# Moving one unit's scores ahead of another unit's products in TensorE's attention order

## The chip, the cores and the metric

The kernel runs on one core of one Trainium2 chip. The metric is the device time of one execution in microseconds (us); lower is better. Three runs of the kernel before are known, and one more execution was recorded by the hardware profiler. In what follows PE is TensorE's matmul row, PEld its weight-load row, DVE is VectorE, ACT is ScalarE, POOL is GpSimd, and SP issues the weight DMAs.

## The reference, cut to what matters

The model is a mixer block followed by two attention blocks, each with a feed-forward block. The change touches only the order of work inside the two attentions. In the first (called "nsa" in the kernel) the part in question is, for each of 16 heads, a masked softmax attention over 512 tokens, computed twice with two sets of keys and values (selected blocks and window; with 512 tokens both are causal attention over all earlier keys). In the second ("swa") it is attention in a band of 128 keys with one sink value per head.

```
def masked_softmax(s, mask):
    s = jnp.where(mask, s, -jnp.inf)
    m = jnp.max(s, axis=-1, keepdims=True)
    p = jnp.exp(s - m)
    d = jnp.sum(p, axis=-1, keepdims=True)
    return p / jnp.where(d > 0.0, d, 1.0)
...
    s = jnp.einsum('bgrqd,bgkd->bgrqk', q_blk, kb) * scale      # scores
    p = masked_softmax(s, mask)                                 # or with the sink in the sum
    o = jnp.einsum('bgrqk,bgkd->bgrqd', p, vb)                  # products with V
...
    o = gates[..., 0, None] * o_cmp + gates[..., 1, None] * o_slc + gates[..., 2, None] * o_win
```

## The kernel before

The whole model is one program, five engine queues written out by hand, with semaphores between them. Outside the attentions TensorE does long rows of 128x512 matmuls on weight tiles that SP streams in, ACT rounds (line 525) and POOL splits (line 494).

An attention is a list of units. A unit is one tile of 128 queries (index i) of one or two pairs of heads, with all key tiles that these queries see. The first attention has 48 units: 8 with one key tile, 8 with two, 16 with three and 16 with four; the first 16 have two pairs of heads, the others one. The second has 16 units of two pairs: 6 with two key tiles, 3 and then 1 with one, then 6 with two. The stages of a unit v and where they stand:

- S(v), function `score` (line 2149, in the second attention also the sinks, line 2153): TensorE multiplies queries with keys into two of the PSUM banks 2 to 5, by the unit's parity. It uses the array as two halves of 64 rows.
- maxima (line 1448), VectorE: adds the mask in place and takes the row maximum.
- E(v), function `exps` (line 799), ACT: exponentials out of PSUM into SBUF, with the row sums.
- T(v), function `turn` (line 2169), TensorE: transposes of the exponentials into banks 6 and 7, again in halves of 64 rows. Behind each half of T(v) stand the transposes W of the row weights of unit v-1 (line 2186).
- the copies of the transposes out of PSUM: bank 6 by VectorE (line 1458), bank 7 by ACT (line 811).
- row weights: VectorE's reciprocal (line 1465), POOL's product with the gates or its spread (lines 428 and 424).
- O(v), function `output` (line 2203), TensorE: V times the transposed exponentials into bank 0 or 1. It uses the array with 128 rows and 64 columns.
- the copy of the turned weights out of PSUM by ACT (line 818), then VectorE's product of output and weights (line 1474), then POOL's sum over branches and its split into high and low parts for the next linear layer.

The order of each queue is fixed. TensorE, in the steady state: T(v+1), O(v), S(v+3), T(v+2). VectorE: maxima(v+3), copy(v+2), reciprocal(v+2), output product(v). ACT: E(v+2), copy(v+1), weight copy(v), E(v+3). T(v+1) waits for E(v+1) and for both copies of unit v; O(v) waits for both copies of unit v; S(v+3) waits until E(v+1) has left its banks; ACT's weight copy(v) waits for O(v). In the second attention VectorE also has parts of the last query tiles between its first units (function `queries`).

The loop on TensorE that sets this order is the last one in `attention` (lines 2219 to 2231):

```
for v in range(v0, last):
    if v + 2 < last:
        score(v + 2)
    ...
    if v + 1 < last:
        turn(v + 1, None if first else v)
    if not first:
        output(v, v + 1 < last)
```

Of the kernel before, what the change touches and what calls it, by code (L numbers as in the profile page):

```python
# [143 lines left out]
def score_columns(i, swa):  # L144

    return P * len(key_tiles(i, swa)) + (1 if swa and i == 0 else 0)


def key_tiles(i, swa):

    return range(max(i - 1, 0), i + 1) if swa else range(i + 1)
# [21 lines left out]
def build(nc, a):  # L173
    with ExitStack() as ctx:
# [1489 lines left out]
        def _(pe):  # L1664
# [123 lines left out]
            def merged_part(stage, j, ks):  # L1788

                w, t = W0[stage] + j, T0[stage] + j  # L1790
                if ks[0] == 0:
                    wait_bank(t)
                    pe.wait_ge(tile_split, w)
                for k in ks:
                    pe.wait_ge(merged, MERGED[stage] + k + 1)
                    mm(psum(BANK[t]), WH[:, w % SPL, k], XH[:, k], start=(k == 0), stop=False)
                    mm(psum(BANK[t]), WH[:, w % SPL, k], XL[:, k], start=False, stop=False)
                    ins = mm(psum(BANK[t]), WL[:, w % SPL, k], XH[:, k], start=False, stop=(k == KT - 1))
                if ks[-1] == KT - 1:
                    ins.then_inc(tile_used, 1)  # L1800
# [327 lines left out]
            def attention(stage, units, v0, swa, lead=None, last_tile=None):  # L2128

                def score(v):  # L2130
                    c, pairs, m, i = units[v - v0]
                    js = key_tiles(i, swa)
                    n, k0 = score_columns(i, swa), P * js[0]
                    K = KS[:, 0] if swa else (KS, KW)[m][:, c // 4]
                    if v - v0 >= 2 or v >= 2 and not swa:
                        pe.wait_ge(p_exp, 2 * (v - 1))
                    if swa:
                        pe.wait_ge(*((q_last, 1) if c == 6 else (freed, T0["swa"] + 2 + c + pairs)))
                        pe.wait_ge(sink_ready, 1)
                    if swa and v == v0 + 1:  # L2140
                        pe.wait_ge(freed, T0["swa"] + 7)

                    s_ = [PS[:, 2 + 2 * (v % 2) + hh, 0:n * pairs].rearrange("p (r n) -> p r n", r=pairs) for hh in range(2)]
                    to = 1 if swa else 0
                    k1 = k0 + P * len(js)
                    for r in range(pairs):
                        for hh in range(2):
                            half = slice(DH * hh, DH * hh + DH)
                            ins = mm(s_[hh][:, r, to:n], QN[half, c + r, P * i:P * (i + 1)], K[half, k1 - n + to:k1],  # L2149
                                     start=(r == 0), stop=(r == pairs - 1 and not swa))  # L2150
                    for hh in range(2 if swa else 0):
                        half = slice(DH * hh, DH * hh + DH)
                        ins = mm(s_[hh][:, :, 0], oneb[half, 0:1].broadcast_to([DH, P]), sink_rows[half, 8 * hh + c:8 * hh + c + pairs],
                                 start=False, stop=True)
                    ins.then_inc(s_mm, 1)

                def turn(v, behind=None):
                    c, pairs, m, i = units[v - v0]
                    js, n = key_tiles(i, swa), score_columns(i, swa)
                    blocks = pairs * len(js)  # L2160
                    for hh in range(2):
                        pe.wait_ge(p_exp, 2 * v + hh + 1)
                        if v >= 1 and hh == 0:
                            pe.wait_ge(pt_d, v)
                            pe.wait_ge(pt_a, v)
                        for b in range(blocks):
                            at, to = n * (b // len(js) + 1) - P * (len(js) - b % len(js)), DH * (blocks * hh + b)
                            for q, rows_ in enumerate(HALVES):
                                ins = nc.tensor.transpose(PS[:, 6 + q, to:to + DH], PE_[rows_, v % 2, hh, at:at + P], ident[rows_, rows_])  # L2169
                        ins.then_inc(pt_mm, 1)  # L2170
                        if behind is not None:
                            if hh:
                                pe.wait_ge(w_half, behind + 1)
                            ins = turn_weight(behind, HALVES[hh])
                            if not hh:
                                ins.then_inc(w_half, 1)

                def turn_weight(v, rows_):
                    if v >= 2:
                        pe.wait_ge(o_done, v - 1)  # L2180
                    if last_tile and v < v0 + 2:
                        pe.wait_ge(freed, T0["swa"] + 9 + v - v0)
                    pe.wait_ge(w_ready, v + 1)
                    for r in range(units[v - v0][1]):
                        to = P * (2 + r)
                        ins = nc.tensor.transpose(PS[:, v % 2, to + rows_.start:to + rows_.stop], WN[rows_, v % 2, r], ident[rows_, rows_])
                    return ins

                def output(v, turned):
                    c, pairs, m, i = units[v - v0]  # L2190
                    pe.wait_ge(pt_d, v + 1)
                    pe.wait_ge(pt_a, v + 1)
                    if not turned:
                        turn_weight(v, slice(0, P)).then_inc(w_half, 1)
                    js = key_tiles(i, swa)
                    blocks = pairs * len(js)
                    for n, j in enumerate(js):
                        V = VW if (j < i if swa else m) else VS
                        for hh in range(2):
                            g = hh if swa else 2 * (c // 4) + hh  # L2200
                            pt = PT_[:, v % 2, :, DH * blocks * hh:DH * blocks * (hh + 1)].rearrange(
                                "p h (r j q) -> p j r h q", r=pairs, q=DH)
                            ins = mm(PS[DH * hh:DH * hh + DH, v % 2, 0:P * pairs].rearrange("p (r h q) -> p r h q", h=2, q=DH), V[:, j, g],  # L2203
                                     pt[:, n], start=(n == 0), stop=(n == len(js) - 1))
                    ins.then_inc(o_mm, 1)

                last = v0 + len(units)
# [6 lines left out]
                if last_tile:  # L2214
                    last_tile()
                    pe.wait_ge(freed, T0["swa"] + 8)
                    pe.wait_ge(tok_out, 6)
                    turn(v0)
                for v in range(v0, last):
                    if v + 2 < last:  # L2220
                        score(v + 2)
                    if v + 2 == last and not swa:
                        pe.wait_ge(p_exp, 2 * (last - 1))
                        merged_part(stage, 0, range(MERGED_PARTS[stage][0]))
                    first = v == v0 and not swa
                    if first:
                        output(v, False)
                    if v + 1 < last:
                        turn(v + 1, None if first else v)
                    if not first:  # L2230
                        output(v, v + 1 < last)
                early, most = MERGED_PARTS[stage]
# [34 lines left out]

            pe.wait_ge(cs_arg, NT)
            attention("nsa_o", NSA_UNITS, 0, False, last_chunk)
            pe.wait_ge(o_done, len(NSA_UNITS))  # L2270
            linear("nsa_o", first=2)
# [3 lines left out]
            pe.wait_ge(down_added, KT)  # L2275
            linear("swa", 9, 4, first=2)
            attention("swa_o", SWA_UNITS, len(NSA_UNITS), True, None, lambda: channel_major("swa", 9, 10))
            pe.wait_ge(o_done, len(NSA_UNITS) + len(SWA_UNITS))
            linear("swa_o", first=2)
# [142 lines left out]
```

## Time and profile before

| | us |
|---|---|
| median of 3 runs | 1599.99 |
| lowest, highest | 1599.51, 1605.58 |
| the profiled execution, whole | 1602.91 |
| its span, first to last instruction | 1601.1 |

The profiled execution is 2.92 us above the median of the runs. A sum made from its rows is taken off its span and, since nothing outside the span changes, off the median as well. Timeline rows are read as: start in us from the span's start, duration in us, engine, line, operation, output and inputs, the array's rows*columns for TensorE, the moving operand, the number of instructions merged into the row, and in brackets the idle time of that engine in front of the row with what ended it. The end of a matmul is modelled, so two matmul rows may overlap by some tenths of a us.

### The profile page before, as it was taken

Reading aid. Unit: us, or ns where it says so; the run is one execution under the profiler, and the core shown is the slowest. Engines: PE = TensorE matmul, PEld = TensorE weight load, DVE = VectorE, ACT = ScalarE, POOL = GpSimd, SP = SyncE. Lnnn points to the kernel's source line nnn. Section 1 sums busy time; section 2 is a strip of 40 time slices with the busy share of each in tenths; the row PEclk is TensorE's granted clock in tenths of the full one; section 3 lists DMA queues with packets and bytes.
Section 4 is the critical chain, followed back from the end, with each engine's and each line's share of the span. In section 5 each row is a group of like instructions: output and inputs, shape, how many; then the busy total and the mean of one; then the engine's idle time right before and its main releaser. Section 6 shows DMA issues by size and latency. Waiting matters only on the chain.

```text
span 1601.1 us, 21978 instructions
## 1 busy us (share of the span) xinstructions
PE 1571.9 (98%) x8401; PEld 1253.0 (78%) x8401; DVE 987.0 (62%) x1590; ACT 625.8 (39%) x1209; POOL 668.6 (42%) x486
## 2 busy tenths in 40 slices
PE   9999999999999999999999999999899999999997
PEld 7888757688888666688888888887668888888886
DVE  5999255567935677676655664457746756556444
ACT  4232334544633677542222222334754222223233
POOL 3444302054422464444444444444454444444443
PEclk9999999999999999999999999999999999999998
DMA  7322201043221000032322323323012232232231
GB/s 266 103 93 92 93 2 52 26 164 119 93 80 61 20 2 2 2 95 102 103 95 93 105 93 107 104 79 105 28 41 92 93 103 96 92 105 93 94 104 54
DMA packets 37817, 133.88 MB, mean 84 GB/s; under 512 B 4752, under 2 KB 5200, under 8 KB 37200
## 3 DMA queue, kind: packets, MB, share of 16 engines
q1 hardware_dynamic: 35840, 125.65, 23.4%
q10 hardware_dynamic: 1872, 6.82, 1.1%
q8 instruction: 68, 1.11, 0.3%
q14 instruction: 37, 0.30, 0.1%
HBM read 130.35 MB, written 2.10 MB: 83 GB/s over the span
## 4 chain that ended last, share of the span: by engine, by line
PE 85%; issue 6%; DVE 4%; ACT 2%; POOL 2%; DMA 0%; DVEq 0%; ACTq 0%; SPq 0%; POOLq 0%
PE ps L1721 17%; PE ps L1723 17%; PE ps L1722 17%; PE ps L2261 5%; PE ps L2263 5%; PE ps L2262 5%; PE ps L2149 2%; PE ps L2203 2%; ACT sb_arena L799 2%; PE ps L1710 1%; PE ps L2169 1%; PE ps L1853 1%; PE ps L1883 1%; PE ps L1906 1%; DVE sb_arena L978 1%
## 5 line engine op out<-in xcount | busy, mean ns | idle before, releaser
L494 POOL TENSOR_TENSOR sb_w_lo<-sb_raw,sb_w_hi 128x1024 fp32r<-128x1024 f32 x224 | 550.6, 2458 | 781.4 <-ACT sb_w_hi L525 734.9
L1721 PE MATMUL ps<-sb_x_hi,sb_w_hi 128*128 128x512 f32 x1280 | 501.8, 392 | 0.6 <-POOL sb_w_lo L494 0.6
L1723 PE MATMUL ps<-sb_x_hi,sb_w_lo 128*128 128x512 f32 x1280 | 498.2, 389 | 0.0
L1722 PE MATMUL ps<-sb_x_lo,sb_w_hi 128*128 128x512 f32 x1280 | 498.0, 389 | 0.0
L525 ACT CAST sb_w_hi<-sb_raw 128x1024 fp32r<-128x1024 f32 x226 | 238.0, 1053 | 637.8 <-PE ps L1723 432.8
L1721 PEld LDWEIGHTS ps<-sb_x_hi,sb_w_hi 128*128 128x128 f32 x1280 | 240.3, 188 | 52.8 <-issue 3.1
L1722 PEld LDWEIGHTS ps<-sb_x_lo,sb_w_hi 128*128 128x128 f32 x1280 | 240.3, 188 | 50.8 <-issue 1.4
L1723 PEld LDWEIGHTS ps<-sb_x_hi,sb_w_lo 128*128 128x128 f32 x1280 | 240.2, 188 | 49.9
L1542 DVE TENSOR_TENSOR sb_x_lo<-sb_arena,sb_x_hi 128x512 fp32r<-128x512 f32 x44 | 98.3, 2242 | 104.8 <-ACT sb_x_hi L864 104.8
L2263 PE MATMUL ps<-sb_x_hi,sb_w_lo 128*128 128x512 f32 x336 | 130.7, 389 | 0.0
L2261 PE MATMUL ps<-sb_x_hi,sb_w_hi 128*128 128x512 f32 x336 | 130.7, 389 | 0.0
L2262 PE MATMUL ps<-sb_x_lo,sb_w_hi 128*128 128x512 f32 x336 | 130.7, 389 | 0.0
L1550 DVE TENSOR_TENSOR sb_arena<-ps,sb_rstd 128x512 f32<-128x512 f32 x44 | 30.4, 691 | 154.7 <-PE ps L1723 154.7
L1554 DVE SCALAR_TENSOR_TENSOR sb_arena<-sb_arena,sb_cols 128x512 f32<-128x512 f32 x44 | 115.8, 2632 | 1.6
L799 ACT ACTIVATE sb_arena<-ps,sb_small 128x256 f32<-128x256 f32 (+4 forms) x192 | 94.0, 501 | 42.6 <-DVE sb_small L1448 34.5
L1448 DVE CUSTOM_DVE_ANT_0 ps<-ps,sb_arena 128x256 f32<-128x256 f32 (+4 forms) x192 | 82.9, 488 | 42.0 <-PE ps L2149 34.2
L859 ACT ACTIVATE sb_arena<-sb_arena 128x512 f32<-128x512 f32 x44 | 27.9, 633 | 150.5 <-DVE sb_arena L1556 150.4
L2263 PEld LDWEIGHTS ps<-sb_x_hi,sb_w_lo 128*128 128x128 f32 x336 | 63.1, 188 | 13.2
L2261 PEld LDWEIGHTS ps<-sb_x_hi,sb_w_hi 128*128 128x128 f32 x336 | 63.1, 188 | 13.0
L2262 PEld LDWEIGHTS ps<-sb_x_lo,sb_w_hi 128*128 128x128 f32 x336 | 63.1, 188 | 13.0
L2169 PEld LDWEIGHTS ps<-sb_ident,sb_arena 64*128 64x128 f32 x864 | 38.9, 141 | 43.8 <-ACT sb_arena L799 37.1
L2149 PE MATMUL ps<-sb_arena 64*128 64x128 f32 (+4 forms) x384 | 65.4, 449 | 0.1
(336 smaller groups left out, 2005.4 us busy)
## 6 DMA issues: line engine op xcount, KB each, us to landing
sb_raw<-in_w SPq DMA_DIRECT2D x227, 512.0 KB, 3.2
sb_arena<-in_cmp_w1k ACTq DMA_DIRECT2D x1, 2048.0 KB, 11.3
sb_arena<-in_cmp_w1v ACTq DMA_DIRECT2D x1, 2048.0 KB, 15.6
out<-sb_resid SPq DMA_DIRECT2D x6, 256.0 KB, 2.3
sb_resid<-in_x SPq DMA_DIRECT2D x5, 256.0 KB, 8.1
sb_arena<-in_pool_w SPq DMA_DIRECT2D x1, 1024.0 KB, 11.7
sb_arena<-in_invc SPq DMA_DIRECT2D x1, 1024.0 KB, 13.6
sb_resid<-in_x ACTq DMA_DIRECT2D x3, 256.0 KB, 7.4
```

Source lines behind the costliest of these rows:

```text
L494: nc.gpsimd.tensor_tensor(WL[:, w % SPL], raw[:, w % RAW], WH[:, w % SPL].bitcast(F32), ALU.subtract).then_inc(tile_split, 1)
L525: nc.scalar.copy(WH[:, w % SPL], raw[:, w % RAW]).then_inc(hi_made, 1)
L799: ins = nc.scalar.activation(PE_[:, v % 2, hh, n * r:n * (r + 1)], PS[:, 2 + 2 * (v % 2) + hh, n * r:n * (r + 1)], ACT.Exp, scale=-1.0, bi ...
L1542: nc.vector.tensor_tensor(XL[:, f % 4], MID[:, f], XH[:, f % 4].bitcast(F32), ALU.subtract).then_inc(xl_ready, 1)
L1554: step.mark(nc.vector.scalar_tensor_tensor(CV[:, b], AP_[:, b, 1:1 + S], w[1], CV[:, b], ALU.mult, ALU.add))
L1721: mm(out, WH[:, s, k], XH[:, k], start=(k == 0), stop=False)
L1722: mm(out, WH[:, s, k], XL[:, k], start=False, stop=False)
L1723: ins = mm(out, WL[:, s, k], XH[:, k], start=False, stop=(k == KT - 1))
L2149: ins = mm(s_[hh][:, r, to:n], QN[half, c + r, P * i:P * (i + 1)], K[half, k1 - n + to:k1], start=(r == 0), stop=(r == pairs - 1 and not swa))
L2261: mm(psum(k), WH[:, s, k], XH[:, x], start=False, stop=False)
L2262: mm(psum(k), WH[:, s, k], XL[:, x], start=False, stop=False)
L2263: ins = mm(psum(k), WL[:, s, k], XH[:, x], start=False, stop=(f == FT - 1))
```

## The change

TensorE's order inside both attentions changes; no operation is added or taken away, and no other engine's program changes. Before, the loop began a turn with the scores of unit v+2. Now the scores of the third unit stand ahead of the loop, and each turn issues the scores of unit v+3 right behind the transposes of unit v+1, in front of the products with V of unit v. In the steady state the order T(v+1), O(v), S(v+3) becomes T(v+1), S(v+3), O(v). In the first turn of the first attention O(0) already stands ahead of T(1), and there nothing moves. The last three turns of an attention have no scores left to issue.

```
@@ -2216,9 +2216,8 @@
                     pe.wait_ge(freed, T0["swa"] + 8)
                     pe.wait_ge(tok_out, 6)
                     turn(v0)
+                score(v0 + 2)
                 for v in range(v0, last):
-                    if v + 2 < last:
-                        score(v + 2)
                     if v + 2 == last and not swa:
                         pe.wait_ge(p_exp, 2 * (last - 1))
                         merged_part(stage, 0, range(MERGED_PARTS[stage][0]))
@@ -2227,6 +2226,8 @@
                         output(v, False)
                     if v + 1 < last:
                         turn(v + 1, None if first else v)
+                    if v + 3 < last:
+                        score(v + 3)
                     if not first:
                         output(v, v + 1 < last)
```

## Rows read from the trace of the kernel before

**Rows 1.** Waits of TensorE: line waiting, releaser: total us, times, longest.

```profile
PE ps L2169 <- ACT sb_arena L811: 13.6, 26, 2.4
```

**Rows 2.** Busy by stretch: length, then PE, PEld, DVE, ACT, POOL busy; clock, DMA.

```profile
544.42:552.05 7.63, 7.02 (x74) 4.68 (x73) 5.33 (x33) 6.04 (x30) 5.98 (x13) 0.90 0.02 3
552.05:577.97 25.92, 23.10 (x271) 15.04 (x270) 20.76 (x89) 21.27 (x81) 16.71 (x34) 1.00 0.01 2
583.29:617.99 34.70, 33.78 (x422) 22.33 (x422) 25.49 (x98) 24.93 (x85) 17.88 (x45) 1.00 0.01 3
617.99:661.96 43.97, 42.04 (x560) 27.53 (x557) 33.19 (x106) 31.23 (x90) 17.38 (x44) 1.00 0.01 2
...
1140.00:1149.00 9.00, 8.12 (x104) 5.52 (x100) 8.90 (x35) 7.39 (x29) 5.12 (x12) 1.00 0.01 4
...
1152.00:1159.56 7.56, 6.93 (x88) 4.70 (x83) 5.50 (x34) 6.10 (x31) 6.02 (x17) 1.00 0.01 3
1159.56:1178.84 19.28, 16.11 (x207) 11.12 (x204) 15.35 (x66) 15.82 (x61) 13.50 (x36) 1.00 0.09 30
```

**Rows 3.** Timeline, one loop of two units with two key tiles, first attention.

```profile
564.77 0.46 PE L2169 MATMUL ps<-sb_ident,sb_arena 64*128 64x64 f32 x8
...
565.65 1.08 PE L2203 MATMUL ps<-sb_arena 128*64 128x256 f32 x8
...
566.66 1.14 PE L2149 MATMUL ps<-sb_arena 64*128 64x256 f32 x8
...
568.81 0.47 ACT L799 ACTIVATE sb_arena<-ps,sb_small 128x256 f32<-128x256 f32 x1 [0.44 <-DVE sb_small L1448]
...
571.09 0.41 ACT L818 COPY sb_arena<-ps 128x256 f32<-128x256 f32 x1
...
571.37 0.46 PE L2169 MATMUL ps<-sb_ident,sb_arena 64*128 64x64 f32 x8
```

**Rows 4.** Timeline, the same loop for units with three key tiles.

```profile
583.29 0.40 PE L2169 MATMUL ps<-sb_ident,sb_arena 64*128 64x64 f32 x6
...
584.79 0.92 PE L2149 MATMUL ps<-sb_arena 64*128 64x384 f32 x4
...
586.47 0.58 ACT L799 ACTIVATE sb_arena<-ps,sb_small 128x384 f32<-128x384 f32 x1 [0.61 <-PE ps L2169]
...
587.34 0.92 PE L2149 MATMUL ps<-sb_arena 64*128 64x384 f32 x4
...
587.60 0.48 ACT L811 COPY sb_arena<-ps 128x384 f32<-128x384 f32 x1
...
588.22 0.40 PE L2169 MATMUL ps<-sb_ident,sb_arena 64*128 64x64 f32 x6
```

**Rows 5.** Timeline, the same loop for units with four key tiles.

```profile
626.69 0.46 PE L2169 MATMUL ps<-sb_ident,sb_arena 64*128 64x64 f32 x8 [0.22 <-ACT sb_arena L811]
...
628.47 1.13 PE L2149 MATMUL ps<-sb_arena 64*128 64x512 f32 x4
...
630.50 0.69 ACT L799 ACTIVATE sb_arena<-ps,sb_small 128x512 f32<-128x512 f32 x1 [1.03 <-DVE sb_small L1448]
...
632.57 0.46 PE L2169 MATMUL ps<-sb_ident,sb_arena 64*128 64x64 f32 x8 [0.22 <-ACT sb_arena L811]
```

**Rows 6.** Timeline, scores with transposes close behind them.

```profile
579.86 0.92 PE L2149 MATMUL ps<-sb_arena 64*128 64x384 f32 x4
...
580.61 0.35 PE L2169 MATMUL ps<-sb_ident,sb_arena 64*128 64x64 f32 x6
```

**Rows 7.** Timeline, the first two full-array matmuls behind scores, second attention.

```profile
1125.25 0.50 PE L1721 MATMUL ps<-sb_x_hi,sb_w_hi 128*128 128x512 f32 x1
1125.59 0.40 PE L1722 MATMUL ps<-sb_x_lo,sb_w_hi 128*128 128x512 f32 x1
```

**Rows 8.** Timeline, start of the second attention.

```profile
1134.97 0.46 PE L2169 MATMUL ps<-sb_ident,sb_arena 64*128 64x64 f32 x8 [2.43 <-ACT sb_arena L811]
...
1137.65 1.05 ACT L525 CAST sb_w_hi<-sb_raw 128x1024 fp32r<-128x1024 f32 x1
```

More of the change, by code:

```diff
@@ L2218, in attention @@
                     turn(v0)
+                score(v0 + 2)
                 for v in range(v0, last):
-                    if v + 2 < last:
-                        score(v + 2)
                     if v + 2 == last and not swa:
@@ L2229, in attention @@
                         turn(v + 1, None if first else v)
+                    if v + 3 < last:
+                        score(v + 3)
                     if not first:
```

## The prediction

> **What bounds the kernel now.** I read three views, from coarse to fine. First the waits of TensorE: nearly all that it waits for by name is ACT's copy of the transposes, 13.6 us in 26 waits, and all of these waits lie in the two attentions [rows 1]. Then the busy time by stretch: in the stretches listed TensorE is idle for 0.61, 2.82, 0.92, 1.93, 0.63 and 3.17 us (length less PE busy; the row from 1140 to 1149 is left out, since it serves another purpose below), 10.1 us in sum [rows 2]. DVE and ACT are less busy than TensorE in each of them, so no engine is full there and something goes round in a loop. Then the timeline, to find that loop.
>
> For units with two key tiles one loop is two units long [rows 3]. T starts at 564.77, O 0.88 later at 565.65, S 1.01 later at 566.66. From S to the start of E is 2.15 (scores, VectorE's maxima of the first head, handover), from E to the transposes that need it 2.56 (ACT's exponentials, then its copy of the unit before, then the handover). Sum 0.88 + 1.01 + 2.15 + 2.56 = 6.60, and the next T of the same parity is at 571.37, 6.60 later. So a unit takes 3.30, and each T of one parity starts when the S of that parity allows it. The same reading for three key tiles gives 1.50 + 1.68 + 1.75 = 4.93, or 2.465 a unit [rows 4], and for four 1.78 + 2.03 + 2.07 = 5.88, or 2.94 a unit [rows 5].
>
> Here the wait rows say too little. At 588.22 T starts with no idle noted, yet ACT's copy ended at 587.60 + 0.48 = 588.08, and T follows it by 0.14; the S in front of it is drawn until 587.34 + 0.92 = 588.26, over the start of T [rows 4]. T could start earlier behind the same S: at 579.86 an S of the same size is followed by transposes after 0.75, not 0.88 [rows 6]. So part of the wait is hidden under the modelled end of S.
>
> **The change, part by part.** No work is added. O(v) and S(v+3) change places. *S waits for nothing new*: its banks are free when E(v+1) is done, and T(v+1), just ahead of it, waited for the same. The moved step issues 4 or 8 matmuls (and two for the sinks), no DMA; it passes nothing on SP's or POOL's queue. What stands behind the moved S on TensorE is O(v), and behind O(v), on ACT, the weight copy(v), and behind that E(v+3). So S now starts where O started, and the loop through S loses O's time: 1.01 of 6.60 with two key tiles. Then one of two others ends last.
>
> *TensorE itself (P).* A unit costs T and O as now (T to S), plus S up to the next T; only the order of the three differs. S up to T is 0.75 for three key tiles [rows 6]; there S is drawn for 0.92, so the overlap is 0.17, and I take S's duration less 0.17 for the others: 1.14 - 0.17 = 0.97 [rows 3] and 1.13 - 0.17 = 0.96 [rows 5], estimates. P is 1.89 + 0.97 = 2.86 with two key tiles, 1.50 + 0.75 = 2.25 with three, 1.78 + 0.96 = 2.74 with four.
>
> *The new wait (Q)*: E(v+3) stands on ACT behind the weight copy(v), which now is released by an O that ends after S. The loop is T to the end of O with S between (T to S as now, S, and the 0.07 by which O is drawn over what follows it: 565.65 + 1.08 against 566.66), 0.05 to the copy (an estimate, below the 0.14 of the handover at 588.08), at most the copy's own 0.41 [rows 3], and E to T. Two key tiles: 1.89 + 0.97 + 0.07 + 0.05 + 0.41 + 2.56 = 5.95, 2.98 a unit. Three: 1.50 + 0.75 + 0.53 + 1.75 = 4.53, 2.27. Four: 1.78 + 0.96 + 0.53 + 2.07 = 5.34, 2.67. So with two key tiles the new wait ends last (2.98), with three it is level with TensorE (2.27), with four TensorE is the bound (2.74). VectorE has 20.76 / 8 = 2.60 of work a unit in the first, 25.49 / 14 = 1.82 and 33.19 / 15 = 2.21 in the others [rows 2]; it fits, closely in the first.
>
> *The sum, by stretch* [rows 2]. 552 to 578, 8 units: 25.92 - 8 x 2.98 = 2.1. 583 to 618, 14 units: 34.70 - 14 x 2.27 = 2.9. 618 to 662, 15 units: 43.97 - 15 x 2.74 = 2.9. The two short stretches of units with one key tile, 544 to 552 and 1152 to 1160, give what TensorE is idle in them, 0.6 each. 1160 to 1179, 6 units of two key tiles and sinks: one S is 0.1 dearer with the sinks, so 3.0 a unit, and the first two have the products of a one-tile unit between them, some 0.3 shorter each; 19.28 - (18.0 - 0.6) = 1.9. Sum 0.6 + 2.1 + 2.9 + 2.9 + 0.6 + 1.9 = 11.0.
>
> Nothing is counted elsewhere. The 2.43 in front of T at 1134.97 [rows 8] stays: the S that this T hangs on keeps its place. Between 1140 and 1149 VectorE is busy 8.90 of 9.0 [rows 2], as it turns the last query tiles beside the units; an earlier S waits for it. There is a small cost too: at 1137.65 ACT rounds a weight tile for 1.05 behind the first weight copy [rows 8], and with the first O now behind an S that rounding and the E behind it come later; I count between 0.4 lost and 0.7 won (VectorE's maxima start earlier) and take none. Clock: from 544.42 to 552.05 the granted clock is 0.90 on the mean [rows 2], so 1.2 GHz for a fifth of that stretch and 2.4 GHz for the rest; TensorE is idle for less after the change, not for more, and I count no change of the clock.
>
> *The price of changing places.* O uses the array as 128 rows by 64 columns, S and T as 64 by 128. Before, the shape changes at T to O and at O to S; after, at S to O and O to T: two in a unit both times. No row shows O behind S. A change of shape costs about 0.20 by the nearest rows: 0.10 since what follows starts 0.07 ahead of the drawn end of O [rows 3] and not 0.17 ahead of S's as without a change [rows 6], and 0.10 since the first full-array matmul behind scores takes 0.50 and the next 0.40 [rows 7]. The bounds are then a net 0.10 gained a unit (T to S without a change, S to O no dearer than S to T) and 0.20 lost (S to O pays, T to S gives nothing back). I take 0, since the two are the same kind of change. The gain of 0.10 in the 29 units that TensorE bounds and half of that in the 14 others would be 3.6 more.
>
> The Trainium skill's page "TensorEngine Tiling (Array Packing)", section "Key Properties", says that changing the tiling mode drains the engine. By it S to O would have to wait for S's whole pipe; the sum would be that of the second rival below instead of mine. The skill's "Perfetto Trace Analysis", section "Identifying the Most-Contended Engine", says that TensorE's matmul busy share measures headroom badly, because pipelined matmuls look different in the trace from what they cost. The rows at 588 agree; by the busy share the sum is that of the first rival.
>
> The sum is off the span of the profiled execution, 1601.1 to 1590.1; that execution stood at 1602.91 as a whole, the median of the runs at 1599.99, so the median goes to **1589.0**. Half a per cent (8.0 us, so below 1592.0 or above 1608.0) is about what a measurement of this kernel can tell from no change.
>
> **The rivals.**
> 1. *Only the idle time that the page shows goes.* If transposes can't start earlier behind S than they are drawn now, the three and four key tiles give 0.9 and 1.9 instead of 2.9 and 2.9: 8.0 in sum, 1592.0. For it: the idle sums [rows 2]. Against it: the 0.75 [rows 6] and the 0.14 at 588.22 [rows 4].
> 2. *The change of shape eats it.* At 0.20 a unit P becomes 3.06, 2.45 and 2.94, the loops through O 3.08 and less: gains 1.3, 0.4 and 0, the short stretches 0.2 each, the last 1.0. Sum 3.1, 1596.9. For it: [rows 7]. Against it: the same price is paid today behind T.
> 3. *Slower, by the same place at a higher price.* TensorE's unit gets dearer than today's loop from about 0.25 a unit on (2.25 + 0.215, 2.74 + 0.20, 2.86 + 0.44). At 0.50, if O must wait for most of the tail of S's last matmul and loads V's weights only then, the units take 3.36, 2.75 and 3.24: losses of 1.0, 3.8 and 4.6, some 1 in each short stretch, 0.9 in the last. Sum -12.3, 1612.3. Against it: no row shows a change at that price.
> 4. *Nothing changes*, since S is held where it stood. Its only wait is that of the T ahead of it, so this needs the order not to reach the chip: 1600.0.
>
> **How the numbers follow.** Forecast 0.62, rival 1 0.16, rival 2 0.13, rival 3 0.06, rival 4 0.03. The predicted time is the forecast's, 1589.0. The range reaches down to 1584.0 (the 3.6 of the free change of shape and the 0.7 and some of the start of the second attention) and up to rival 2's 1596.9; it leaves out rivals 3 and 4 and a little at each end. Faster by over 0.5%: most of the forecast and half of rival 1, 0.66. Within: the rest of these, rivals 2 and 4, 0.28. Slower: rival 3, 0.06.
>
> **What would show it.** In the profile after, with three key tiles, two units after two units follow in about 4.5 instead of 4.93, and TensorE's waits for ACT's copy are gone there; with two key tiles E should start right behind ACT's weight copy, not behind VectorE's maxima, and T come every 2.98. The wait of 2.43 should stand. Each stretch should be shorter by its term. If T still follows ACT's copy by 0.14 with three and four key tiles, P isn't the bound and the loop has another member; if O starts more than 0.1 behind the drawn end of S, the change of shape is what I sized wrong.

## The result and the profile after

| | before | after |
|---|---|---|
| median of the executions shown side by side (4 and 4), us | 1599.75 | 1582.38 |
| lowest, highest | 1598.34, 1605.58 | 1582.33, 1584.37 |
| profiled execution: span, mean granted clock | 1601.1, 0.992 | 1580.5, 0.997 |

The ratio is 0.9888 (95% interval 0.9862 to 0.9913): 17.4 us faster, where the forecast was 11.0 and its range ended at 1584.0. Two later sets of the same changed kernel, each against the kernel before on its own chip, gave 1585.26 (ratio 0.9910, 0.9893 to 0.9927) and 1585.01 (0.9908, 0.9894 to 0.9921). So the change is worth between 13.5 and 17.4 us from set to set. Of the twelve executions of the changed kernel in these three sets, three stand at 1582.4 and the other nine between 1584.4 and 1586.4. Below, 14.5 of the first set's 17.4 is traced to the order and the rest to TensorE's clock.

The waits of TensorE after the change (line waiting, releaser: total us, times, longest):

```profile
PE ps L2169 <- ACT sb_arena L811: 7.9, 10, 2.4
...
PE ps L2186 <- POOL sb_arena L428: 1.1, 3, 0.4
```

13.6 us in 26 waits [rows 1] have become 7.9 in 10. The longest, 2.4 at the start of the second attention, stands as forecast, and a small one has grown from 0.3 to 1.1: the transposes of the weights now wait for POOL (0.39 each) in two units of one key tile too.

Busy by stretch after (columns as in [rows 2]), cut at the same transposes: third to fourth, fourth to fifth, fifth to eighth, eighth to sixteenth, eighteenth to 32nd, 32nd to 47th of the first attention; then third to seventh, seventh to tenth, tenth to sixteenth of the second:

```profile
536.26:538.20 1.94, 1.90 (x25) 1.28 (x25) 1.58 (x10) 1.79 (x10) 0.60 (x2) 1.00 0.00 0
538.20:540.39 2.19, 1.95 (x24) 1.33 (x25) 2.06 (x15) 2.18 (x11) 1.65 (x4) 1.00 0.00 0
540.39:547.12 6.73, 6.26 (x72) 4.17 (x73) 5.35 (x32) 5.93 (x30) 5.75 (x14) 1.00 0.01 4
547.12:570.28 23.16, 21.91 (x271) 14.75 (x269) 21.61 (x91) 21.47 (x81) 17.08 (x35) 1.00 0.01 2
575.43:606.83 31.40, 31.40 (x424) 21.03 (x422) 27.24 (x99) 24.89 (x84) 18.09 (x45) 1.00 0.01 3
606.83:647.13 40.30, 40.30 (x561) 26.35 (x560) 35.44 (x107) 31.24 (x90) 17.64 (x45) 1.00 0.01 2
1122.90:1135.27 12.37, 10.64 (x154) 7.80 (x153) 11.62 (x45) 11.24 (x41) 7.00 (x17) 1.00 0.01 3
1135.27:1142.20 6.93, 6.51 (x84) 4.49 (x83) 6.08 (x37) 6.13 (x30) 6.04 (x17) 1.00 0.02 4
1142.20:1159.12 16.92, 15.38 (x204) 11.11 (x203) 15.23 (x65) 16.10 (x61) 13.46 (x36) 1.00 0.10 34
```

With three and four key tiles TensorE has no idle time left: 31.40 of 31.40 and 40.30 of 40.30. The two loops that the forecast named, for two key tiles and for three (timeline rows; the last two of the second are a product and its next transposes with four key tiles):

```profile
558.77 0.46 PE L2169 MATMUL ps<-sb_ident,sb_arena 64*128 64x64 f32 x8
...
559.56 1.08 PE L2149 MATMUL ps<-sb_arena 64*128 64x256 f32 x7
...
560.57 1.08 PE L2203 MATMUL ps<-sb_arena 128*64 128x256 f32 x8
...
561.70 0.37 ACT L818 COPY sb_arena<-ps 128x256 f32<-128x256 f32 x1 [0.23 <-PE ps L2203]
...
561.97 0.48 ACT L799 ACTIVATE sb_arena<-ps,sb_small 128x256 f32<-128x256 f32 x1
...
563.78 0.60 ACT L811 COPY sb_arena<-ps 128x512 f32<-128x512 f32 x1
...
564.52 0.46 PE L2169 MATMUL ps<-sb_ident,sb_arena 64*128 64x64 f32 x8
```

```profile
593.25 0.40 PE L2169 MATMUL ps<-sb_ident,sb_arena 64*128 64x64 f32 x6
593.37 0.27 ACT L818 COPY sb_arena<-ps 128x128 f32<-128x128 f32 x1 [0.46 <-PE ps L2203]
...
593.53 0.59 ACT L799 ACTIVATE sb_arena<-ps,sb_small 128x384 f32<-128x384 f32 x1
...
593.77 0.97 PE L2149 MATMUL ps<-sb_arena 64*128 64x384 f32 x4
...
594.65 0.49 ACT L811 COPY sb_arena<-ps 128x384 f32<-128x384 f32 x1
594.67 0.88 PE L2203 MATMUL ps<-sb_arena 128*64 128x128 f32 x12
595.48 0.46 PE L2169 MATMUL ps<-sb_ident,sb_arena 64*128 64x64 f32 x7
...
629.78 1.09 PE L2203 MATMUL ps<-sb_arena 128*64 128x128 f32 x16
630.81 0.46 PE L2169 MATMUL ps<-sb_ident,sb_arena 64*128 64x64 f32 x8
```

In the first, T at 558.77, the end of O at 560.57 + 1.08 = 561.65, the weight copy at 561.70, E right behind it at 561.97, ACT's copy until 564.38, and the next T of the parity 0.14 later, at 564.52: 5.75 for two units, and the wait for the weight copy is in it. In the second a unit takes 595.48 - 593.25 = 2.23, and T comes 0.34 behind ACT's copy (594.65 + 0.49 = 595.14), not 0.14 as before [rows 4]: ACT is early there, and TensorE is the bound.

### The profile page after: what moved, and what is told of

Same layout as the page of the kernel before. It is cut to its first block, busy times and chain, and to the rows that moved or that the text cites. A ratio compares the mean times of both kernels' runs of the same rounds, so it can differ in the third digit from the quotient of the medians.

```text
span 1580.5 us, 21978 instructions
## 1 busy us (share of the span) xinstructions
PE 1557.3 (99%) x8401; PEld 1244.1 (79%) x8401; DVE 992.7 (63%) x1590; ACT 625.1 (40%) x1209; POOL 667.7 (42%) x486
## 4 chain that ended last, share of the span: by engine, by line
PE 87%; issue 4%; DVE 4%; ACT 2%; POOL 2%; DMA 0%; SPq 0%; DVEq 0%; ACTq 0%; POOLq 0%
PE ps L1721 18%; PE ps L1723 18%; PE ps L1722 18%; PE ps L2263 5%; PE ps L2262 5%; PE ps L2264 5%; PE ps L2203 3%; PE ps L2149 2%; PE ps L2169 2%; PE ps L1710 1%; DVE sb_arena L978 1%; ACT sb_arena L799 1%; PE ps L1853 1%; PE ps L1883 1%; PE ps L1906 1%
## 5 line engine op out<-in xcount | busy, mean ns | idle before, releaser
L2203 PE MATMUL ps<-sb_arena 128*64 128x128 f32 (+1 forms) x656 | 61.0, 316 | 0.0
```

## The experiments

### Is the extra gain at the starts the clock's, and does the order set it?

In the profiled execution of before TensorE stands at half clock, 1.2 GHz, from 539 to 546 and from 1136 to 1140; after the change it stands at 2.4 GHz in both places. I call such a stretch at half clock a fall. The two starts of before, third to fifth transposes of the first attention and second to third of the second:

```profile
538.40:544.42 6.02, 6.02 (x49) 4.19 (x51) 2.84 (x16) 4.22 (x21) 2.59 (x4) 0.56 0.00 0
1134.97:1139.20 4.23, 4.23 (x38) 2.74 (x40) 1.04 (x4) 3.48 (x11) 0.40 (x1) 0.67 0.00 0
```

They shrank by 1.9 and 1.4 us, and I had counted nothing there. Theory C: the order of the first turns keeps the clock up. Rival R: the falls belong to single executions. Four kernels ran side by side on one chip.

New order in the first turns only:

```
+                    ahead = v0 + (1 if swa else 2)
-                    if v + 2 < last:
+                    if v + 2 < last and (v == v0 or v > ahead):
                         score(v + 2)
...
+                    if v < ahead:
+                        score(v + 3)
```

> The kernel before, with the new order only in the second turn of the first attention (S(4) ahead of O(1)) and the first turn of the second attention (S(3) ahead of O(0)); all later turns in the old order. Theory C (the clock): of the 6.5 us that the forecast missed, some 3 come from TensorE no longer falling to 1.2 GHz at the two starts, and it is the order of these first turns that decides it. Then the granted clock is 1.00 from the first transposes on in both attentions, the stretch of three units behind the third transposes of the first attention is shorter by about 1.8, the unit behind the second transposes of the second attention by about 1.3, and the time is 3 to 4 us below the kernel before (about 1596). Rival R (the fall belongs to one execution, not to the order): the clock falls as in the kernel before, and the gain is under 1 us.

The complement: old order first (`if v <= late: score(v + 2)` at the loop's start, `if late <= v < last - 3: score(v + 3)` behind the transposes, with the same limits):

> The complement: the first turns keep the old order (first attention up to the second turn, second attention the first), and from the next turn on S stands ahead of O as in the changed kernel. Theory C: the clock falls again at both starts, and the time is 3 to 4 us above the changed kernel, about 1586. Rival R: the clock does what it does whatever the order, and the time stays within 1 us of the changed kernel, 1582 to 1583.5.

Old order with idle time filled (`fill` is called behind `score(v + 2)`, once in each attention):

```
+                def fill(bank, count):
+                    if swa:
+                        pe.wait_ge(freed, T0["swa"] + 9)
+                    K = KS[:, 0]
+                    for k in range(count):
+                        half = HALVES[0]
+                        mm(PS[:, bank, 0:2 * P], QN[half, 0, 0:P], K[half, 0:2 * P], start=True, stop=True)
...
+                    if v == v0 + (0 if swa else 1):
+                        fill(0 if swa else 1, 7 if swa else 3)
```

> The kernel before in its old order, with extra score matmuls of one array half, whose results nobody reads, in TensorE's idle times at the two starts: 3 ahead of the third transposes of the first attention (idle 0.91 before), 7 ahead of the second transposes of the second (idle 2.43 before). Theory C: with the idle time filled the clock stays at 1.00 and the first attention's start gains about 1.7, the second's about 1.2, together some 3 us, without any change of order: about 1597. Rival L (the gain at the starts is the shorter loop and not the clock): no gain, 1599 to 1600.5, even if the clock stays up.

The kernel before, unchanged:

> The kernel before once more, unchanged, to see whether its two stretches at half clock (539 to 546 and 1136 to 1140) come back in another execution. Theory C: both are there again, at the same work, and the mean granted clock of every execution is about 0.993 to 0.995, below the 0.996 to 0.997 of the changed kernel. Rival R: at least one is missing or stands elsewhere, and the mean clock scatters up to 0.997.

Measured: first turns only 1598.05 (ratio to before 0.9999, 0.9989 to 1.0008), complement 1585.76 (0.9919, 0.9905 to 0.9934), filled 1598.88 (0.9998, 0.9989 to 1.0008), before again 1600.07, all against 1599.74. By times alone the complement gave C's number, while the first turns and the filled kernel missed C's 1596 and 1597. The profiles say what the complement's time does not. Before again, the stretches of [rows 2] and, first, the third to fifth transposes:

```profile
536.34:541.05 4.71, 4.02 (x48) 2.75 (x49) 3.47 (x21) 3.99 (x21) 2.37 (x4) 1.00 0.00 0
541.05:548.30 7.25, 6.71 (x73) 4.37 (x73) 4.88 (x30) 6.12 (x31) 6.28 (x15) 1.00 0.01 3
...
1131.18:1135.70 4.52, 4.52 (x38) 2.88 (x40) 1.04 (x4) 3.49 (x11) 0.40 (x1) 0.62 0.00 0
1135.70:1148.51 12.81, 11.15 (x157) 7.97 (x154) 12.36 (x49) 10.24 (x40) 7.06 (x17) 1.00 0.01 3
```

The same kernel has no fall at the start of the first attention here: third to fifth transposes take 4.71, not 6.02, the stretch behind them 7.25 at 1.00, not 7.63 at 0.90 [rows 2]. The fall at the second start is back (0.62). First turns only has that one too, although its work in the second attention up to the fall is the changed kernel's. So R: the order doesn't decide it. The kernel with the idle time filled shows no fall at either start; it stands 1.2 below before again, not the 3 that C gave it.

### The changed kernel again, shifted, and filled

The rival now is alignment (theory A): the fall depends on where the work stands when it idles, not on its order. Unchanged, then a third time beside the last two filled kernels:

> The changed kernel once more, unchanged. Theory A (alignment): whether the clock falls at the start of the second attention isn't fixed by the order but by where the work stands when it idles; since the executions of one kernel stand nearly alike, most executions of the changed kernel again show no fall: mean clock 0.996 to 0.997, 1582.0 to 1582.8, and the unit from the second to the third transposes of the second attention takes 2.81. Rival C (order): none of the executions shows a fall.

> The changed kernel a third time, beside the two filled kernels. Theory A: the fall at the start of the second attention is there in some executions of this kernel and not in others: the times stand in groups near 1582.4 (mean clock 0.997) and 1585 (0.995), as the two earlier sets do, and the gain against the kernel before lies between 13.5 and 17.4 us. Rival C: all executions agree with the first set, 1582.4.

Shifted: in `output`, `for n, j in [*enumerate(js)] * (2 if not swa and v in (40, 41) else 1):`

> The changed kernel with the products O of two units of the first attention (numbers 40 and 41, four key tiles) issued twice, so that all that follows, the second attention's start too, stands some 2.1 us later; order and work at that start are untouched. Theory A (alignment): the price is 2.1 us plus or minus 1 to 2.5 us of clock, since the fall at the start of the second attention and the last fall at the end of the program land elsewhere; if the fall comes back, the unit from the second to the third transposes of the second attention takes about 3.8 to 4.4 instead of 2.81. Rival C (order): the price is 2.1 within 0.3, 1584.5, and that unit stays at 2.81.

Filled, with 7 and then 5 extra matmuls at the second start (as `fill` does, in the changed order; each `mm` stands in the trace as two instructions), and the old order with 5 there:

> The changed kernel with TensorE's idle time ahead of the second transposes of the second attention filled by 7 extra score matmuls of one array half, whose results nobody reads, as was done with the old order. With the clock up at that start in both, the difference to the filled kernel in the old order is the order's own worth. Theory A: about 14.5 to 15 us (11.0 in the first attention, 4.0 in the second), so 1582.4 to 1584.0 here, beside 1598.9. Rival C (the order gives 17.4 by itself): 1581.5 or below.

> As after_filled, the changed kernel with TensorE's idle time at the start of the second attention filled, but with 5 extra matmuls instead of 7: seven take 2.83 us and held the transposes behind them up by some 0.6, five should end by 0.3 before these. Theory A (alignment): the clock stays at 1.00 at that start in every execution, the unit from the second to the third transposes takes 2.8, and the time is below that of the changed kernel of the same call by what the fall costs there (1.4) if it has one, and level with it if not: 1582 to 1583.5. Rival C: the extra work changes nothing that counts, and the time is that of the changed kernel within 0.5.

> The kernel before, old order, with the same 5 extra matmuls at the start of the second attention alone. With the clock up at that start in both, after_filled5 less filled5 is the worth of the order alone. Theory A: 14.5 to 15 us, of which 11.0 in the first attention and 3.4 behind the third transposes of the second; the unit from the second to the third transposes of the second attention takes 2.9 to 3.4 here. Rival C: 17 us or more.

Filled at both starts, with 2 and 5:

> The changed kernel with TensorE's idle time filled at both starts: 5 extra matmuls of one array half ahead of the second transposes of the second attention, as before, and 2 ahead of the third transposes of the first, where TensorE is idle for 0.91 (one such matmul takes about 0.4, so they end just before). Theory A (a fall needs the idle time and is placed by alignment): no execution falls at either start; the first attention's second to fourth unit take 4.1 to 4.3, the second attention's second unit 2.8, and the time is 1581.8 to 1582.8, the best of all kernels here. Rival I (the fall at the first attention's start comes from the idle times further on or before, 0.36 and 0.2, and isn't reached by the fill): the fall at 538 stays in part of the executions, and the time is 1584 to 1585.

| kernel | median, us | second to third transposes, second attention | fall, first start | fall, second start |
|---|---|---|---|---|
| after, first set | 1582.38 | 2.81 | no | no |
| after again | 1585.26 | 4.22 | no | yes |
| after, third set | 1585.01 | 2.82 | yes | no |
| shifted | 1587.17 | 4.40 | no | yes |
| after, 7 extra | 1584.24 | 3.33 | no | no |
| after, 5 extra | 1584.42 | 2.81 | yes | no |
| old order, 5 extra | 1597.84 | 2.88 | yes | no |
| after, 2 and 5 extra | 1583.94 | 2.81 | no | no |

The falls are those of the profiled executions. The rows behind them (columns as before), the second to third transposes of the second attention in after and in after again:

```profile
1120.09:1122.90 2.81, 2.81 (x38) 2.07 (x38) 1.94 (x9) 2.17 (x9) 0.40 (x1) 1.00 0.00 0
```

```profile
1120.09:1124.31 4.22, 4.22 (x38) 2.67 (x39) 2.68 (x12) 2.16 (x9) 0.40 (x1) 0.64 0.00 0
```

and the third to fifth transposes of the first attention with that place of the second, in the third set:

```profile
536.66:542.59 5.93, 5.93 (x49) 3.86 (x50) 3.93 (x23) 3.85 (x20) 2.87 (x5) 0.56 0.00 0
1122.24:1125.06 2.82, 2.82 (x38) 2.08 (x39) 1.94 (x9) 2.17 (x9) 0.40 (x1) 1.00 0.00 0
```

The second start of after and after again begins at the same 1120.09 with the same instructions, and one runs at 1.00 and the other at 0.64. So one kernel shows the fall at the second start, at the first, or at neither; it costs 1.4 at the second and 1.8 (5.93 against 4.13) at the first. C is out, and so is its reading of the complement's 1585.76: that is where the changed kernel itself stands in two sets of three. Theory A's own expectations failed as well: after again was to stand at 1582.0 to 1582.8 without the fall, and the third set was to split into groups at 1582.4 and 1585, where all four of its executions stand at 1584.84 to 1585.85. That the fall follows alignment is argued, not shown: the shifted kernel has it, but so has the unshifted one run beside it, so the shift tells nothing (it costs 1.9 between the medians, 1.74 by the doubled products). One more sign for A is in the profiles: of the twelve that leave the first start open, the five that fall there begin the first attention's transposes at 530.88 or later, the seven others at 530.78 or earlier; but no run set that time. In none of the five profiles filled at the second start, nor of the two filled at the first, does the clock fall where the idle time is filled. Left open, six of nine fall at the second start and five of twelve at the first. That the filling is what kept the clock up is not shown all the same: each kernel was profiled in one execution, and with the start left open some show no fall either. Seven extra matmuls were too many, they end behind ACT's copy and the unit takes 3.33; five cost nothing in the changed order (2.81).

The worth of the order, free of the clock, comes from pairs of profiles without a fall in the same place. First attention, first to 48th transposes, in before again and in after; second, first to sixteenth, in the old and in the new order with 5 extra:

```profile
530.77:664.30 133.53, 124.99 (x1525) 82.74 (x1525) 98.27 (x388) 97.69 (x343) 66.95 (x152) 1.00 0.02 5
530.70:653.25 122.55, 119.00 (x1525) 79.41 (x1524) 103.35 (x388) 97.40 (x343) 66.82 (x152) 1.00 0.02 6
```

```profile
1127.90:1174.53 46.63, 40.96 (x512) 29.07 (x511) 38.31 (x170) 38.68 (x151) 27.49 (x70) 1.00 0.04 14
1117.39:1160.47 43.08, 39.28 (x511) 28.58 (x511) 38.90 (x170) 38.80 (x151) 27.29 (x70) 1.00 0.04 15
```

That is 10.98 and 3.55, in sum **14.5**. The other profiles of the changed order without a fall there agree: 122.58 (after again) and 122.59 (2 and 5 extra) in the first attention, 43.14 (third set) in the second. The medians of the two kernels with 5 extra differ by only 13.4, their profiled executions by 14.4; both of these show a fall at the first start, which costs the old order 0.6 and the new 0.9.

The first set's 17.4 is 14.5, plus 1.4 for the fall that before has at the second start (in both its profiles; in before again it costs 1.6) and after has not, plus 1.3 in the tail: from the last transposes to the end 422.74 in before again, 421.40 in after. There too the clock falls before the end, and in after it fell later relative to the work. No other of the fourteen profiles has a tail under 421.90, so this part belongs to the execution as well. The version with 2 and 5 extra matmuls, whose clock stayed up at both starts, has that tail at 422.69; its 1583.94 is 1.1 to 1.3 below the changed kernel's two later sets, not the 1582 I expected, and no better than the first set. Its ratio to before (0.9900, 0.9883 to 0.9916) isn't clear of theirs, so no gain of the fill is shown.

### Which bound holds in which unit?

ACT's weight copy in pieces, nothing else changed:

```
-                    nc.scalar.copy(WB[:, v % 2, 0:pairs], PS[:, v % 2, 2 * P:2 * P + P * pairs].rearrange("p (r q) -> p r q", q=P)
-                                   ).then_inc(w_copied, 1)
+                    for r in range(pairs):
+                        for q in range(0, P, P // 4):
+                            ins = nc.scalar.copy(WB[:, v % 2, r, q:q + P // 4], PS[:, v % 2, P * (2 + r) + q:P * (2 + r) + q + P // 4])
+                    ins.then_inc(w_copied, 1)
```

> The changed kernel with ACT's weight copy cut into pieces of 32 columns: 8 for units of two pairs of heads, 4 for units of one. By the rows after the change a copy of 256 columns delays the exponentials behind it by 0.27 and one of 128 by 0.16, so some 0.05 an instruction and 0.11 per 128 columns (an estimate): 0.62 in 8 pieces, 0.31 in 4. Theory Q (with two key tiles the loop through O, the weight copy and E ends last; with three and four TensorE does): the eight units behind the eighth transposes of the first attention take 23.16 + 8 x 0.175 = 24.6, the last six of the second attention 16.9 + 1.0 = 17.9, and the units of three and four key tiles stay at 2.23 and 2.72; some 3 us in all. Rival P (TensorE is the bound everywhere): no stretch changes by more than 0.2.

1591.38 (0.9951, 0.9935 to 0.9968), 6.1 above after again beside it, where theory Q gave some 3. By stretch, the eighth to sixteenth, 18th to 32nd and 32nd to 47th transposes of the first attention:

```profile
549.36:573.96 24.60, 21.84 (x269) 14.64 (x270) 21.64 (x90) 24.43 (x141) 16.86 (x33) 1.00 0.01 2
579.11:610.85 31.74, 31.53 (x423) 21.11 (x422) 27.23 (x99) 27.71 (x130) 18.17 (x45) 1.00 0.01 3
610.85:651.15 40.30, 40.30 (x560) 26.34 (x558) 35.44 (x107) 34.01 (x135) 17.69 (x45) 1.00 0.01 2
```

Two key tiles: 24.60, as theory Q said, so the new wait on the weight copy ends last there. Four: 40.30, not a hundredth changed. Three: 0.34 in all, of which 0.33 stands in the first unit (2.56 for 2.23; most likely the last copies of two pairs, which was not tried by itself); nearly all others stay at 2.23. The last six units of the second attention took 18.43, dearer than the 17.9 I gave; with pieces their units of 2.58 to 2.90 all became 3.01 to 3.18. What else went beyond the 3 stands in stretches that the expectation left out: third to tenth transposes of the second attention 1.2 longer (units with two key tiles, then with one), and third to eighth of the first 2.1, part of it a fall (mean clock 0.87).

That TensorE is the bound with four key tiles has a second witness in the shifted kernel: doubling two products there made the stretch 42.04 for 40.30, 0.87 for each. One such unit, where O stands as 32 matmuls for 16:

```profile
634.15 1.16 PE L2149 MATMUL ps<-sb_arena 64*128 64x512 f32 x4
635.24 1.97 PE L2203 MATMUL ps<-sb_arena 128*64 128x128 f32 x32
637.14 0.46 PE L2169 MATMUL ps<-sb_ident,sb_arena 64*128 64x64 f32 x8
```

## Why the prediction was too small

The direction and the mechanism were right; the size was off by 6.4 us in the first set. Two steps failed. In the sum over the order the new wait Q was priced too dear (2.98 a unit with two key tiles, measured 2.88 to 2.90; 2.27 with three, where TensorE's 2.23 holds) the units with four key tiles came 0.8 cheaper in sum than P gave, and three stretches stood at nothing: 11.0, where the order gave 14.5. And *"I count no change of the clock"* left out the 2.9 beyond it. I set the sum against what the order alone gave: before again and the old order with 5 extra, less after and after with 5 extra.

| stretch | forecast | measured | why |
|---|---|---|---|
| first attention, 3rd to 5th transposes | 0 | 0.58 | not in the sum |
| 5th to 8th | 0.6 | 0.52 | |
| 8th to 16th (two key tiles) | 2.1 | 2.76 | Q too dear |
| 16th to 18th | 0 | 0.17 | not in the sum |
| 18th to 32nd (three) | 2.9 | 3.30 | Q taken, P holds |
| 32nd to 47th (four) | 2.9 | 3.68 | P fits; first two units |
| second attention, 2nd to 7th | 0 | 0.51 | taken as 0 between -0.4 and 0.7 |
| 7th to 10th | 0.6 | 0.64 | |
| 10th to 16th | 1.9 | 2.39 | Q too dear |
| sum (what is left out gives -0.02) | 11.0 | 14.5 | |

- *"So S now starts where O started"* and *"Then one of two others ends last"*: right. T, S, O follow each other as forecast, and which of P and Q holds was right for two and four key tiles.
- *Q with two key tiles, 2.98*: the term that failed by size. Measured 5.75 / 2 = 2.88 (over the eight units 23.16 / 8 = 2.90). T to the end of O is 2.88 and not 2.93, and above all the copy delays E by 0.27 (561.70 to 561.97), not by its drawn 0.41. I used the drawn length as an upper end and let it stand as the value; I had the pipelining of neighbours on TensorE in the sum and not on ACT.
- *Q with three key tiles, 2.27*: here I charged the copy of two pairs (0.41) to units of one pair, whose copy delays E by 0.16 (593.37 to 593.53). With that Q is below P, and P, 2.25, comes within 0.02 of the 2.23 measured. 14 units of 0.04 are the missing 0.4 less 0.2 in the last of them, which already has a four-tile S.
- *P with four key tiles, 2.74*: measured 2.72. The 0.8 missing is 13 times 0.02 and the first two units, which I priced at 2.74 and which take 2.43 and 2.51, as they still have transposes or products of three key tiles.
- *Stretches counted at nothing*: 1.3 us (0.58, 0.17 and 0.51). The units with one key tile ahead of the first row of [rows 2] hold idle time like those in it (4.71 less 4.02 in before again); I left the stretch out, since there the clock was low and the idle time hidden under stretched matmuls.
- *The price of changing places, taken as 0*: right. With three key tiles S to O is 594.67 - 593.77 = 0.90, 0.15 more than S to T [rows 6]. T to S is 0.52 and O to T 0.81, in sum 1.33, where T to O to S took 1.50 [rows 4]: 0.17 comes back, and a unit gets 0.02 cheaper by the order. So rivals 2 and 3 fall, and with them what I had worked out from the Trainium skill's page "TensorEngine Tiling (Array Packing)", section "Key Properties", that a change of mode drains the engine: S to O costs 0.15 more than S to T, but the new order has as many changes as the old.
- *"I count no change of the clock"*: the step that carried the first set out of the range. I read the half clock of one profiled execution as a property of the kernel. It is one of the execution: of the 2.9 beyond the order's 14.5, 1.4 to 1.6 is a fall at the second start and 1.3 the fall in the tail. The 1601.1 of the span held two more such stretches, at the first start and, from 10 to 13 us, at the program's own, worth some 2 each; before again has neither, and its span is 1598.1. The Trainium skill's page "TensorE: Matmul & The Clock Gate", section "Part 1: The HAM clock gate", says that how many matmuls at a kernel's start run at the low clock varies between runs of one kernel. The runs here show such a variation in the middle of the program too (0.64 against 1.00 at the same 1120.09).
- *Rival 1, only the shown idle time goes*: out. The stretches with three and four key tiles lost 3.30 and 3.68 where they showed 0.92 and 1.93 idle [rows 2]. *Rival 4*: out.
- *"nearly all that it waits for by name is ACT's copy"*: 13.6 of 20.5 us over the whole program, so two thirds; the sum doesn't hang on it.
- The two later sets, 1585.26 and 1585.01, lie inside the range of 1584.0 to 1596.9, the first set doesn't. The order alone, 1599.99 less 14.5, gives 1585.5: inside too, though the sum was 3.5 short of it.

## What to carry to other kernels

When a step moves from between two engines' loop into a place where it waits for nothing, price the loops that remain by the distance from start to start of neighbours in the trace, on every engine, and take each operation's size from the unit that it is used in: drawn lengths overstated the new wait by 0.1 to 0.25 here. Look at the granted clock of the stretch before you take a time from it, and profile the kernel before a second time: a stretch at half clock may belong to the execution, and then it neither bounds the change nor repays it. A difference of one to three us at such places is not the edit's until the clock is equal on both sides.

## What the runs showed of the hardware

- The granted clock of the same instructions at the same moment of the program was 1.00 in one execution and 0.64 over the stretch in another (after and after again at 1120.09); the unit took 2.81 and 4.22. In none of five profiles did the clock fall at that start where its idle time was filled with matmuls that nobody reads, in six of nine it did where it was open.
- An O right behind an O costs 0.87 (1.74 for two, shifted kernel), where O to T between other shapes takes 1.03 (629.78 to 630.81 in after): 0.16 more, which I put down to the change of the array's shape.
- On ACT a copy of 256 columns delays what follows by 0.27, one of 128 by 0.16, while they are drawn for 0.37 and 0.27; eight copies of 32 columns took 0.63 (561.35 to 561.98, weight copy in parts).
